# Turned input, scale behind the projections, and an earlier release of gathers in a two-layer decoder step

## The reference, cut to what matters

```python
u = rmsnorm(h, norm_mix[0])            # h * rsqrt(mean(h*h) + eps) * g, per token
zxbcdt = u @ w_in                      # z 2048 | x,B,C 4096 | dt 32
xbc, new_buf = causal_conv(xbc, conv_buf, conv_w, conv_b)   # 4 taps over time
xbc = silu(xbc); dt = softplus(dt + dt_bias)
y, h_state = ssd_scan(xs, dt, a, bm, cm, h0)   # chunks of the prompt; states of the samples
y = norm(y * silu(z)) ; h = h + y @ w_out
...
# PEER, per token: 8 heads pick 16 of 16384 experts each (two top-16 lists of 128 keys,
# then the top 16 of their 256 sums)
act  = gelu(einsum('td,thkd->thk', xb, expert_u[idx]))
out  = einsum('thk,thkd->td', softmax(best_s) * act, expert_v[idx])
```

## Time and profile before

| | us |
|---|---|
| median of 3 runs | 2444.46 |
| lowest and highest | 2441.75, 2446.61 |
| profiled execution | 2444.89 |
| its span | 2443.1 |
| busy: PE, VectorE, POOL, ScalarE | 1741.4, 1569.0, 1340.1, 260.7 |

### The profile page before, as it was taken

One profiled execution on the slowest core, in us unless ns is written; L12 is line 12 of the kernel. 1 busy time (PEld: TensorE's weight loads), 2 busy tenths in 40 slices (PEclk: granted clock), 3 DMA queues, 4 the chain that ended last, 5 costly groups with the idle time before them and its releaser, 6 DMA issues.

```text
span 2443.1 us, 22858 instructions
## 1 busy us (share of the span) xinstructions
PE 1741.4 (71%) x7437; PEld 762.4 (31%) x7437; DVE 1569.0 (64%) x3812; ACT 260.7 (11%) x628; POOL 1340.1 (55%) x1496
## 2 busy tenths in 40 slices
PE   7999799494406666678788676886756767556678
PEld 4577658334400010022335223451213412001112
DVE  2388777999798757652644898878765644733321
ACT  2133212001000000011110111110011100000000
POOL 0011653266547777755665556665645664677774
PEclk9999899596756666689889887787877978699999
DMA  4332257399979999999999999999999999999997
GB/s 162 111 131 70 94 181 257 119 407 417 417 268 407 420 420 419 420 409 416 416 419 416 413 415 364 419 416 417 416 414 420 408 415 386 396 419 420 419 419 294
DMA packets 270247, 859.09 MB, mean 352 GB/s; under 512 B 26288, under 2 KB 31344, under 8 KB 270128
## 3 DMA queue, kind: packets, MB, share of 16 engines
q0 software_dynamic: 184320, 671.17, 67.9%
q1 hardware_dynamic: 85808, 186.46, 20.3%
HBM read 845.26 MB, written 12.17 MB: 351 GB/s over the span
## 4 chain that ended last, share of the span: by engine, by line
POOL 23%; DMA 18%; PE 11%; issue 9%; DVE 8%; ACT 0%; SPq 0%; POOLq 0%; DVEq 0%; ACTq 0%
POOL arena L2491 23%; DMA arena<-peer_v,arena 11%; PE banks L880 4%; DVE arena L2137 3%; PE banks L1072 3%; DMA wring<-w_q 2%; DMA arena<-peer_u,arena 2%; DMA wring<-ple_w_gate 1%; DMA wring<-peer_w_query 1%; PE banks L820 1%; DMA wring<-w_o 1%; PE banks L989 1%; DVE arena L1951 1%; PE banks L558 1%; DVE arena L1948 1%
## 5 line engine op out<-in xcount | busy, mean ns | idle before, releaser
L2137 DVE SCALAR_TENSOR_TENSOR arena<-arena,banks 128x1024 f32<-128x1024 f32 x640 | 763.1, 1219 | 451.5 <-DMA arena<-peer_u,arena 445.1
L1072 PE MATMUL banks<-arena 128*32 128x512 f32 x2560 | 703.5, 726 | 383.3 <-DMA arena<-peer_v,arena 376.9
L2491 POOL DMA_INDIRECT arena<-peer_u,arena x640 | 606.2, 947 | 386.2 <-issue 186.4
L2491 POOL DMA_INDIRECT arena<-peer_v,arena x640 | 607.4, 949 | 351.1 <-issue 173.4
L1072 PEld LDWEIGHTS banks<-arena 128*32 128x32 f32 x2560 | 93.7, 117 | 870.3 <-DMA arena<-peer_v,arena 704.9
L880 PE MATMUL banks<-wring,uT 128*128 128x512 f32 (+3 forms) x448 | 217.5, 634 | 40.7 <-DMA wring<-w_q 17.8
L558 PE MATMUL banks<-cst,arena 128*128 128x128 f32 (+2 forms) x349 | 61.3, 330 | 147.3 <-DVE arena L2153 82.2
L634 PE MATMUL banks<-uT,wring 128*128 128x320 f32 x512 | 139.1, 433 | 0.0
L880 PEld LDWEIGHTS banks<-wring,uT 128*128 128x128 f32 (+1 forms) x448 | 78.0, 184 | 188.2 <-issue 153.5
L2424 POOL COPY arena<-arena 128x3 f32<-128x3 f32 x32 | 6.0, 188 | 207.5 <-ACT arena L1416 207.5
L634 PEld LDWEIGHTS banks<-uT,wring 128*128 128x128 f32 x512 | 96.7, 190 | 39.8 <-issue 0.4
(11 more groups left out here) (270 smaller groups left out, 1883.2 us busy)
## 6 DMA issues: line engine op xcount, KB each, us to landing
wring<-peer_w_query SPq DMA_DIRECT2D x40, 1024.0 KB, 18.4
wring<-ssm_w_in SPq DMA_DIRECT2D x24, 1024.0 KB, 7.2
wring<-w_q SPq DMA_DIRECT2D x18, 1024.0 KB, 20.4
wring<-ssm_w_out SPq DMA_DIRECT2D x16, 1024.0 KB, 9.1
wring<-ple_w_gate SPq DMA_DIRECT2D x12, 1024.0 KB, 12.2
arena<-peer_u,arena POOLq DMA_INDIRECT x640, 11.6
arena<-peer_v,arena POOLq DMA_INDIRECT x640, 9.9
out_sample_ssm<-arena SPq DMA_DIRECT2D x16, 512.0 KB, 3.8
```

The lines of the kernel that those rows point to most:

```text
L1072: mm = pe.matmul(sums(t, at, half), place_of(t, at), rows_buf[:, k, half * 512:(half + 1) * 512], start=at < spots(t), stop=False, skip_gr ...
L2137: dve.scalar_tensor_tensor(rows_buf[:, k, :], rows_buf[:, k, :], 1.0, u_now, ALU.mult, ALU.mult, accum_out=pact[:, n % 2, at:at + 1]).then ...
L2491: pool.indirect_dma_start(rows_buf[:, k, :], None, tables[kind], bass.IndirectOffsetOnAxis(ap=rows, axis=0))\
```

## The change

1. The program gets x a second time, turned on the host (`x_T`, channels on the partitions), and the gain as a column per 128 channels (`gain_T`). SP loads both first, in two halves with the first two weights between, then h, the constants and the dt weights. VectorE multiplies the gain into uT. The transposes, the gain row and u are gone; the square sums stay.
2. 1/rms is applied behind the projections: in tanh's scale and the gate's product, in dt, and for x, B, C as a row over the tokens, made by three matmuls of ones with a diagonal and copied by ScalarE (`rstd_row`). VectorE's product of the bank with that row replaces ScalarE's copies into `raw`.
3. PE runs gate block 0 ahead of the norm row and of dt.
4. The picks advance by 2, 2, 1, 0, 0 in turns 3 to 7, so that one quad is picked in the scan; `first_select` waits 15 steps in place of 8 on PE and ScalarE.
5. The block rows `bm` are made by POOL in place of VectorE, ahead of `ctm`; its wait for `ec` moves ahead of them.
6. "scan_over" is told behind the last states, ahead of `scale_rows` and `turn_rows`; POOL also waits for ScalarE's last square.

```diff
@@ tensor
+                    if n == 0:
+                        pe.wait_ge(*dve_done.at(("input", half)))
...
+            gate_block(0)
             pe.wait_ge(*cst_in.at("cst"))
-            norm_transposes("mix0")
+            pe.wait_ge(*dve_done.at("rstd_diag"))
+            acc = claim(pe, "rstd_row")
+            for t in range(3):
+                mm = pe.matmul(acc[:, OFF[t]:OFF[t] + ROWS[t]], ones[0:ROWS[t], :], rstd_diag[0:ROWS[t], t, 0:ROWS[t]],
+                               start=True, stop=True)
+            mm.then_inc(*full("rstd_row"))
...
-            gate_block(0)
...
-                pe.wait_ge(*dve_done.at(("bm", g)))
+                pe.wait_ge(*pool_done.at(("bm", g)))
...
             def first_select():
-                for _ in range(8):
+                for _ in range(15):
                     yield
@@ sync
+            sp.dma_start(uT[:, 0:4, :], I["x_T"][:, 0:4, :]).then_inc(x_in[0].sem, 16)
+            sp.wait_ge(*dve_done.at("small"))
+            sp.dma_start(gainT, I["gain_T"]).then_inc(gainT_in.sem, 16)
+            load_weights(sp, 1)
+            sp.dma_start(uT[:, 4:8, :], I["x_T"][:, 4:8, :]).then_inc(x_in[1].sem, 16)
+            load_weights(sp, 2)
...
-            load_gain(0, "mix0", I["norm_mix"][0:1, :])
...
-            load_weights(sp, 2)
+            load_weights(sp, 4)
@@ scalar
-            norm("mix0", lambda t: h_in[t].at("x"))
-
+            for t in ALL:
+                square("mix0", t, h_in[t].at("x"))
+            bank = filled(act, "rstd_row")
+            freeing(act.activation(rstd_row, bank[:, 0:NTOK], ACT.Copy), "rstd_row")
...
-                bank = filled(act, ("xbc", b))
-                act.wait_ge(*pool_done.at(("rawstate", b)))
-                s(act.activation(raw[:, b % 4, 3:259], bank[:, 0:256], ACT.Copy))
-                freeing(act.activation(raw[:, b % 4, 259:347].rearrange("p (b w) -> p b w", b=8)[:, :, 3:11],
-                                       bank[:, 256:320].rearrange("p (b w) -> p b w", b=8), ACT.Copy), ("xbc", b))
@@ vector
-            norm("mix0", 0)
+            dve.wait_ge(gainT_in.sem, 16)
+            for half in range(2):
+                dve.wait_ge(x_in[half].sem, 16)
+                part = uT[:, 4 * half:4 * half + 4, :]
+                s(dve.tensor_tensor(part, part, spread(gainT[:, 4 * half:4 * half + 4], NTOK), ALU.mult), dve_done, ("input", half))
+            dve.wait_ge(*squares.at(("mix0", 2)))
+            s(dve.tensor_scalar(var[:, 0:3], ssq[:, 0:3], 1.0 / D, EPS, ALU.mult, ALU.add))
+            rsqrt(rstd[:, 0:3], var[:, 0:3], nwt[:, 0:3])
...
-                    s(dve.tensor_scalar(zz, zz, 0.5, 0.5, ALU.mult, ALU.add))
+                    s(dve.tensor_scalar(zz, zz, 1.0, half_rstd[0:ROWS[t], t:t + 1], ALU.add, ALU.mult))
...
+            def take_block(b):
+                bank = filled(dve, ("xbc", b))
+                dve.wait_ge(*pool_done.at(("rawstate", b)))
+                s(dve.tensor_tensor(raw[:, b % 4, 3:259], bank[:, 0:256], rstd_row[:, 0:256], ALU.mult))
+                of_seq = lambda v: v.rearrange("p (b w) -> p b w", b=8)
+                freeing(dve.tensor_tensor(of_seq(raw[:, b % 4, 259:347])[:, :, 3:11], of_seq(bank[:, 256:320]),
+                                          of_seq(rstd_row[:, 256:320]), ALU.mult), ("xbc", b))
...
             def conv(b):
-                dve.wait_ge(*freed(("xbc", b)))
+                take_block(b)
...
                 if g >= 3:
-                    advance(early_picks, (3, 3, 2, 2, 2)[g - 3])
-
-            def block_rows(g):
-
-                if g >= 2:
-                    dve.wait_ge(*full_at(("hupd", 2 * g - 3, 1)))
-                elif g == 0:
-                    dve.wait_ge(*full_at("ec"))
-                s(dve.tensor_tensor(bm[:, g % 2, :, :], repeat(btok[:, 2, g * 128:(g + 1) * 128], 4),
-                                    spread(cst[:, C_SEQ:C_SEQ + 4], 128), ALU.mult), dve_done, ("bm", g))
+                    advance(early_picks, (2, 2, 1, 0, 0)[g - 3])
...
                 if t == 2:
                     new_states(g)
+                    if g == GROUPS - 1:
+                        tell("scan_over")
...
             turn_rows(2)
-            tell("scan_over")
@@ gpsimd
                 if t == 2:
+                    pool.wait_ge(*freed("ec"))
+                    s(pool.tensor_tensor(bm[:, g % 2, :, :], repeat(btok[:, 2, g * 128:(g + 1) * 128], 4),
+                                         spread(cst[:, C_SEQ:C_SEQ + 4], 128), ALU.mult), pool_done, ("bm", g))
...
             pool.wait_ge(*dve_done.at("scan_over"))
+            pool.wait_ge(*act_done.at(("gsq", 2, GROUPS - 1)))
```

More of the change, by code:

```diff
@@ L288, in build @@
         bcT = area(6144, 16, NTOK)
+        rstd_row = area(15360, NTOK)
+        rstd_diag = area(15680, 3, 128)
+        half_rstd = small[:, 1208:1211]
+        gainT = small[:, 1212:1220]
         xs = [area(11264, D_INNER), area(11264 + D_INNER, D_INNER), area(29440, D_INNER)]
@@ L463, in build @@
         rows_in = signal("conv_rows_loaded")
+        x_in = [signal(f"turned_input_loaded{i}") for i in range(2)]
+        gainT_in = signal("turned_gain_loaded")
         dtw_in = signal("dt_weights_loaded")
@@ L1224, in store_state @@
                              hnew[:, blk % 2, :, :]).then_inc(*hnew_out[blk % 2].mark(blk, 16))
-            for t in range(3):
-                for half in range(2):
-                    sp.wait_ge(*full_at(("uT", "mix0", t, half)))
+            sp.wait_ge(*squares.at(("mix0", 2)))
             def load_state(blk):
@@ L1393, in _ @@
                     if t < 2:
-                        s(act.activation(z[:, t, n * 512:(n + 1) * 512], bank, ACT.Tanh, scale=0.5), act_done, ("ztanh", n, t))
+                        s(act.activation(z[:, t, n * 512:(n + 1) * 512], bank, ACT.Tanh, scale=half_rstd[:, t:t + 1]),
+                          act_done, ("ztanh", n, t))
                     else:
@@ L1397, in _ @@
                             s(act.activation(z[0:64, 2, n * 512 + 256 * c:n * 512 + 256 * c + 256],
-                                             bank[64 * c:64 * c + 64, 0:256], ACT.Tanh, scale=0.5), act_done, ("ztanh", n, 2))
+                                             bank[64 * c:64 * c + 64, 0:256], ACT.Tanh, scale=half_rstd[64 * c:64 * c + 64, 2:3]),
+                              act_done, ("ztanh", n, 2))
             def conv_tanh(b):
@@ L1821, in _, with gate @@
             s(dve.memset(small[:, :], 0.0), dve_done, "small")
-            norm("mix0", 0)
+            dve.wait_ge(gainT_in.sem, 16)
[6 more added lines that the diff above has]
+            rsqrt(rstd[:, 0:3], var[:, 0:3], nwt[:, 0:3])
+            s(dve.tensor_copy(rstd[64:128, 2:3], rstd[0:64, 2:3]))
+            s(dve.tensor_scalar(half_rstd, rstd[:, 0:3], 0.5, None, ALU.mult), dve_done, "half_rstd")
+            dve.wait_ge(*cst_in.at("cst"))
+            for t in range(3):
+                s(dve.tensor_scalar(rstd_diag[:, t, :], ident, rstd[:, t:t + 1], None, ALU.mult),
+                  *((dve_done, "rstd_diag") if t == 2 else ()))
+            def gate(n):
+                for t in range(3):
+                    zz = z[0:ROWS[t], t, n * 512:(n + 1) * 512]
+                    dve.wait_ge(*act_done.at(("ztanh", n, t)))
+                    s(dve.tensor_scalar(zz, zz, 1.0, half_rstd[0:ROWS[t], t:t + 1], ALU.add, ALU.mult))
+                    bank = filled(dve, ("z", n, t))
+                    if t < 2:
+                        freeing(dve.tensor_tensor(zz, zz, bank, ALU.mult), ("z", n, t))
+                    else:
+                        s(dve.tensor_tensor(zz[:, 0:256], zz[:, 0:256], bank[0:64, 0:256], ALU.mult))
+                        freeing(dve.tensor_tensor(zz[:, 256:512], zz[:, 256:512], bank[64:128, 0:256], ALU.mult), ("z", n, t))
             dve.wait_ge(vec_in.sem, 48)
@@ L1826, in _ @@
                 bank = filled(dve, ("dt", t))
-                freeing(dve.tensor_tensor(dt[:, t, :], bank[:, 0:32], dtb_bc, ALU.add), ("dt", t))
+                freeing(dve.scalar_tensor_tensor(dt[:, t, :], bank[:, 0:32], rstd[:, t:t + 1], dtb_bc, ALU.mult, ALU.add), ("dt", t))
             s(dve.scalar_tensor_tensor(dtmp, dt, -1.0, dt, ALU.mult, ALU.max), dve_done, "dt_abs")
@@ L1840, in _ @@
             for n in range(4):
-                for t in range(3):
-                    zz = z[0:ROWS[t], t, n * 512:(n + 1) * 512]
-                    dve.wait_ge(*act_done.at(("ztanh", n, t)))
-                    s(dve.tensor_scalar(zz, zz, 0.5, 0.5, ALU.mult, ALU.add))
-                    bank = filled(dve, ("z", n, t))
-                    if t < 2:
-                        freeing(dve.tensor_tensor(zz, zz, bank, ALU.mult), ("z", n, t))
-                    else:
-                        s(dve.tensor_tensor(zz[:, 0:256], zz[:, 0:256], bank[0:64, 0:256], ALU.mult))
-                        freeing(dve.tensor_tensor(zz[:, 256:512], zz[:, 256:512], bank[64:128, 0:256], ALU.mult), ("z", n, t))
+                gate(n)
```

(9 more changed lines are left out.)

5 lines of the change are left out of this document (3 added, 2 removed).

## The result

The changed kernel takes 2449.94 us (median; 2444.95 to 2456.86), the kernel before 2445.57 on the same chip: a ratio of 1.0020, with a 95% interval of 1.0012 to 1.0027. It is slower, by 0.2% or 4.9 us (2.9 to 6.6), where 7.7 us faster was forecast. The profiled execution has a span of 2447.9 us against 2443.1, and 1.8 around it.

A forecast was written before the change was run, and what follows sets the result against it. From 721.6 us the DMA engines are full, so the first expert phase's end moves the kernel's end: -4.2+11.5-22+7 = -7.7 us, 2437 us. The forecast's own range was 2430 to 2443, the whole range 2422 to 2452.

The forecast's parts named there:

- head, to PE's last gate block: PE starts at 8.5 us, stands 8.1 ahead of gate block 1, starts slowly (2.2), ends gates at 97.7: 4.2 earlier.
- convolution, to the last silu: VectorE gets two products per block, needs 4.96 us each and becomes the bound: 11.5 us later (8 to 14).
- scan, to VectorE's first memset of the expert phase: Late sample turns take some 9 us in place of 15.5, so VectorE is through 22 us earlier (14 to 26).
- first expert phase, from that memset to its end: First 128 gathers and dot products: 20.5 us more picks, less 19.6 of old waits, plus 6 left: 7 us longer.
- rest: From 721.6 us to the end the DMA engines are full and nothing changes, so the shift is kept: 0.
- The balance that I set up: First expert phase: DMA at 406 GB/s has the first 96 blocks' share by 630, VectorE reaches block 96 at 632.
- the scan's paragraph: Samples' scan: gathers go at 459.9 and fill 14 slots while VectorE finishes, so its first waits go.
- The replay: Scan turns replayed from 399.5 with the trace's intervals: turn 5 starts near 428.5, last states told at 455.0 before the shift.
- The third: First expert phase: PE's late scores keep VectorE waiting, phase 20.5 us longer, 5.8 slower in all, 2451; chance 0.15.
- The first, all waits covered: First expert phase only 1 us longer, scan 26 earlier with the late turns at their best: 2427; chance 0.22.
- The second, VectorE starting 14 us earlier: Scan: last turns keep 12 us each because stores land late behind loads; no change, 2445; chance 0.20.
- The shared port: Scan: POOL's block rows could stop VectorE products with two SBUF inputs, up to 2 x 1.1 us; nothing was added.

The follow-up runs named there:

- work_early: The kernel before with 12 VectorE instructions of 0.69 us that change nothing, behind dot products 12 to 23 of the first expert phase; 2452.9 us.
- work_late: The kernel before with the same 12 VectorE instructions that change nothing, behind dot products 80 to 91 of the first expert phase; 2449.2 us.
- picks_spread: The changed kernel with seven empty steps between the picks of the third and fourth quad, and 22 for 15 in PE's and ScalarE's waits; 2440.0 us.
- picks_back: The changed kernel with the picks as before (3, 3, 2, 2, 2 steps in turns 3 to 7, wait of 8 steps); 2452.7 us.
- gate_first: The changed kernel with the tanh and products of gate block 0 ahead of the dt chain on ScalarE and VectorE; 2439.6 us.

## Why the prediction was wrong, point by point

| term | forecast | measured, changed against before |
|---|---|---|
| head, to PE's last gate block | -4.2 | -2.8 (101.94 to 99.2) |
| convolution, to the last silu | +11.5 | +11.2 |
| scan, to VectorE's first memset of the expert phase | -22 | -17.2 (-8.7 behind +8.5) |
| first expert phase, from that memset to its end | +7 | +12.6 (236.8 to 249.4) |
| rest | 0 | +1.0 |
| sum | -7.7 | +4.8 |

**The step that failed** is the first expert phase: "Against that stand VectorE's 19.6 us of waits for gathers in this phase", of which 13.6 were to go. Only 7.6 went, 19.6 to 12.0. The other term of this sum, 20.5 us of picks, was about right: VectorE is busy for 19.5 us more, and the 12.6 of the table with the 7.6 make 20.2. (The 23.4 us that an expectation above names add up instruction times that overlap.) What was wrong is that the waits were taken as one sum. In the trace of before they lie at the first four dot products (4.6 us) and behind the dot product 72 (15.0), while the moved picks lie between the first and about the 56th. From the dot product 4 to the dot product 56 it takes 112.7 us in place of 91.2, and only behind it, from 72 to 96, are some us won back, 36.4 in place of 44.6. The balance that I set up, DMA and VectorE both at block 96 near 630, held only if the DMA never stood. But with 14 slots the gathers can't run further ahead of a late VectorE: between 485 and 660 us POOL waited 59.3 us for dot products, where it was 43.0, and in 540 to 610 us the DMA share fell to 0.86. VectorE came to block 96 at 657.6, that is 181.5 us behind its memset, not 169. work_early and work_late show this with added work alone, and picks_spread wins back 8.2 us by place alone. The first waits, which the scan's paragraph let go because the gathers would fill 14 slots in time, stayed for the most part: 3.3 of 4.6 us. VectorE got to its first dot product 7.0 us behind the first gather, and one gather takes about as long from issue to landing (the second, issued at 474.52, was waited for until 481.65); in picks_back it got there 11.1 us behind, and had no first waits.

A second term was mis-sized, within its bounds: the scan gave 17.2 us in place of 22. (In the kernels with the changed scan, the stretch from the last silu to the memset varied by 4.3 us, so part of the difference may be chance.) The replay had the last state told at 455.0, with the shift 462.3; it is 467.6. Its first gather, 459.9, is 4.9 us behind that tell and not the 3.9 that it names; no term of the sum hangs on this. Turn 5 began at 438.65, 2.9 later than the replay and its shift, and behind it the states were told 13.3 and 8.7 us apart, not 9 and 9. The two terms together were to give 15 us and gave 4.6. picks_back puts the reason in one pair of numbers: the picks' move alone brought the memset 15.0 us forward and made the stretch from it to the end of the phase 15.3 longer.

**The rivals.** The third had the time nearly right (2451), but by luck: its phase is 20.5 longer where 12.6 were measured, its scan 22 shorter where 17.2 were, and these two errors offset each other in part. Its mechanism, PE's scores so late that VectorE waits for them, is not what happened: PE ends the scores at 656.5, VectorE takes them up at 658.8, at block 96, where the steps put it, and has waited for gathers alone. The first, all waits covered, falls with 12.0 us of them left. The second, VectorE starting 14 us earlier, is nearer than the forecast's 22 on the scan. The 12.6 lie within the bounds that I had written down for the phase, 1 to 20.5; between ends that far apart I took 7 on a balance of totals, and the balance was the mistake.

**What held.** The head's mechanism: PE at 8.35 (8.5 said), 8.31 us of standing (8.1), and dt at the higher level of the clock for nearly all of it (5.18 for 4.5, not 8.9). The first block took 20.5 us and the three others 55.9 for 53.7 and a slow start of 2.2, as summed. But the standing is not the whole cause of that start: the granted clock had fallen to 0.50 (1.2 GHz) by 34.5 us, with dt still running, and stood there until 47; in gate_first it fell as well, without any standing. The convolution: 0.42 and 0.22 us for the two products and 4.94 a block were said to 0.02.

**The shared port.** I added nothing for products that POOL might stop. The last two turns show some: four products of 64x256 of VectorE took 1.53, 0.77, 0.93 and 1.56 us, where this size takes 0.42: 3.1 us more in all. Three of them, below what POOL ran beside them:

```profile
451.28 1.90 POOL L2500 TENSOR_TENSOR arena<-u,small 128x1024 f32<-128x1024 f32 x1 [1.61 <-DMA out_sample_ssm<-arena]
...
460.28 3.94 POOL L2500 TENSOR_TENSOR arena<-arena,small 128x1024 f32<-128x1024 f32 x2 [3.28 <-DMA out_sample_ssm<-arena]
```

```profile
451.92 1.53 DVE L1948 TENSOR_TENSOR arena<-arena 64x256 f32<-64x256 f32 x1 [1.51 <-ACT arena L1451]
...
461.52 0.93 DVE L2090 TENSOR_TENSOR arena<-arena 64x256 f32<-64x256 f32 x1
462.49 0.41 DVE L2092 TENSOR_TENSOR arena<-arena,banks 64x256 f32<-64x256 f32 x1
462.94 1.56 DVE L2094 TENSOR_TENSOR arena<-arena 64x256 f32<-64x256 f32 x1
```

The three shown began while POOL scaled the old states, not while it made the block rows, and the product between them, which takes one input from PSUM, has its usual 0.41. (One product of turn 5 did begin beside the block rows, which POOL made from 439.14 to 440.24: at 439.62, and it took 0.89 us.) That is as the Trainium skill has it (SBUF — State Buffer, Who interferes with whom): a VectorE product with two SBUF inputs meets GpSimd's reads, one with at most one SBUF input does not. The trace agrees, but it explains no difference: from turn 3 to the memset, VectorE's instructions took 9.0 us in all beyond the shortest of their line and shape, and 8.2 before the change. Block rows made on VectorE again were not tried.

## What to carry to other kernels

A sum of waits is no store of time: ask where in the stretch the waits lie and where the added work lies, and how far ahead the buffers let the supplier run (here 14 slots). Added work kept nearly its full price ahead of the waits (8.1 of 8.8 us) and almost none in them (0.6). Work that is moved from one place where an engine sets the pace to another where the same engine does so gains little or nothing (here 15.0 us earlier, 15.3 us longer), so look for the place where that engine waits. A scale that stands behind a projection was cheaper here multiplied once into its input, where the old use of this input is over, than into each block of the result: two products of 1.49 us for 32 times 0.73, with ScalarE, which had time, copying the blocks.

## What the hardware showed that I had not expected

A gather that POOL issues takes 0.94 us, but the first one took 2.83 us in the changed kernel and 1.14 before. In the changed kernel it began half a us after a VectorE product of 64x2048 with two SBUF inputs (470.90 to 473.18) and ended 1.0 us behind it. The traces of the experiments tell what this hangs on: in all nine kernels in which the first gather begins beside that product it takes 2.81 to 2.85 us, and in the five others 1.14 or 1.15. One of the five is hold_release, which is the changed kernel with the gathers told later:

```profile
473.44 1.15 POOL L2520 DMA_INDIRECT arena<-peer_u,arena  x1 [12.65 <-issue]
```

Smaller products show it as well: a gather of the changed kernel that began at 499.41, beside a product of 128x512 with two SBUF inputs (499.33 to 500.02), took 1.42 us. So the early release ran into `scale_rows`, and 1.7 us of the lead went there. What in the product holds a gather was not tried.
